# A hybrid decoder step: the token mixer of the next tile divided into pieces and placed between the expert groups of the present tile

## The chip, the cores and the metric

The kernel runs on one core of a Trainium2 chip. The metric is the device time of one execution in microseconds (us). The core's engines work side by side and meet through semaphores: TensorE (PE; its weight loads are listed as PEld), VectorE (DVE), ScalarE (ACT), GpSimd (POOL) and SyncE (SP). Sixteen DMA engines move data between HBM and the on-chip memory.

## The reference, cut to what matters

One decoder layer is computed for 1024 prompt tokens and for 8 sample tokens (one new token of each of 8 sequences with a cache). All data are float32, the width is 1024.

```
h   = rmsnorm(x) * (1 + sc1) + sh1                 # six modulation vectors from silu(c) @ w_ada + b_ada
rq, rk, rv, rg, aq, ak, av = split(h @ w_in)       # 7 x 512 columns, 8 heads of 64 each
ret = groupnorm(retention(rq, rk, rv)) * silu(rg)  # chunks of 128 tokens, state carried from chunk to chunk
att = dilated_window_attention(norm(aq), norm(ak), av)   # softmax with counts and distances, over all earlier tokens
x   = x + gt1 * (concat(ret, att) @ w_out)
h2  = rmsnorm(x) * (1 + sc2) + sh2
for each of 8 heads of each token:                 # product-key experts
    s1, s2 = the two halves of (h2 @ w_pq) times sub_keys;  16 best sums s1[i] + s2[j] -> 16 experts, gates g
    y += sum over the 16 experts of  g * gelu(u_e . h2) * v_e
x   = x + gt2 * y
```

Outputs are the new rows of the prompt and of the samples, the retention states, and the keys and values. The attention of a tile needs the keys of all earlier tiles, and the retention needs the state left by the tile before. The experts of a token need only its own h2.

## The kernel before, in words

The tokens are worked on in 8 tiles of 128 (`T = 8`). Three functions follow one another, each a block that ends with all engines meeting.

`front` first computes the modulation: twelve chunks of w_ada of 2 MiB stream through three buffers (L207, L527). It then runs the mixer in a loop over the 8 tiles. For each tile, nine chunks of 2 MiB (7 of w_in, 2 of w_out, 512 columns each) stream through the same three buffers; the products are L577 (w_in) and L662 (w_out). TensorE makes the score products (L608) of a head, VectorE adds the distances and takes the maximum (`att_max`, L420), ScalarE takes the exponential (L314), TensorE turns the probabilities (L633), VectorE multiplies them by the counts (`att_weigh`, L431), and TensorE makes the weighted sum of the values (L647). Two pairs of PSUM banks hold the scores of two heads. The number of keys is rounded up to a multiple of 256. At the end of a tile the residual `x_mid` and the normed row `h2` are stored to HBM (L251, L252).

`decode` does the mixer of the 8 sample rows, with its own pass over w_in and w_out and a gathered part of the cache.

`peer` does the experts. Queries, turned queries and scores of a head are made by TensorE four heads ahead (L1259, L1265, L1270), and VectorE chooses the 16 experts two heads ahead, in eight parts (`choose_next`, L1368 to L1412). A row of `uv` holds an expert's u and v, 8 KB. GpSimd gathers one expert for each of the 128 tokens into one of eight ring buffers (`gather`, L1145), 1 MiB at a time, 16 times a head. The ring is used in groups of two slots:

```
for q in range(GROUPS):                     # 8 groups of a head; 8 heads, 8 tiles: 512 groups
    DVE : wait gathered;  dot[s] = sum(ring[s][u] * h2)      # L1448, twice
    ACT : act_h = gelu(dot)                                  # L1230
    DVE : act_h = act_h * gate / sum(gates)                  # L1457
    DVE : one of the eight parts of the choice for head n + 2
    ACT : ring[s][v] = ring[s][v] * act_h[s]                 # L1190, twice
    PE  : psum += turned ring[s][v], 8 blocks                # L1325; then the two slots are free
    POOL: wait free;  gather two more
```

Every engine runs its part of this in its own written order. At the end of a tile VectorE waits for the sum (L1337), scales it, TensorE turns it back (L1342), and VectorE adds it to `x_mid` (L1464, L1468); SP stores y (L1136) and loads the next h2 (L1132). The loops over tiles and heads are loops of the engines.

## Time and profile before

| | us |
|---|---|
| median of 3 runs | 3856.61 |
| lowest and highest | 3854.44, 3859.69 |
| the profiled execution | 3865.25 |
| its span, first to last instruction | 3863.6 |
| TensorE, VectorE, ScalarE, GpSimd busy | 2684.1, 2437.5, 1676.4, 1270.9 |
| mean granted TensorE clock (1 is 2.4 GHz) | 0.827 |

Busy time counts the instructions of an engine that compute; the idle time before an instruction is put down to whoever released it. The DMA share is the mean busy share of the sixteen DMA engines. A span is from the first to the last instruction, so the profiled execution's own time is a little longer.

### The profile page before, as it was taken

What the parts mean: (1) busy time and instruction counts of PE and PEld (TensorE: products, weight loads), DVE (VectorE), ACT (ScalarE), POOL (GpSimd) and SP (SyncE); (2) the same over time, 40 slices, a digit from 0 to 9 for tenths busy, and PEclk for the clock granted to TensorE, in tenths of its full rate; (3) what the DMA queues carried; (4) which work ended last, traced back from release to release, by engine and by line L of the source; (5) the groups of instructions that cost most, each with busy time, mean ns of one, the idle gap of its engine ahead of it and who ended that gap; (6) DMA issues with size and microseconds to landing.
All of it is one profiled execution on the core that took longest, in us unless ns stands there. A gap on an engine that the chain in (4) does not pass through costs nothing.

```text
span 3863.6 us, 42539 instructions
## 1 busy us (share of the span) xinstructions
PE 2684.1 (69%) x13275; PEld 1978.7 (51%) x13275; DVE 2437.5 (63%) x5982; ACT 1676.4 (43%) x2367; POOL 1270.9 (33%) x1089
## 2 busy tenths in 40 slices
PE   8999999999666656666656666665666566566656
PEld 2445545555124555555555555555555555555554
DVE  0333234444137777777777777777777777777776
ACT  0221122222104555555455555555555555555553
POOL 0000000000003544444444444444544444444443
PEclk9888899999878878777778787778878777787778
DMA  8566665543748999999999999999999999999998
GB/s 305 207 223 223 223 221 201 193 155 128 263 170 328 421 401 398 422 401 421 393 420 407 407 422 404 422 396 402 422 398 422 401 422 406 406 422 400 422 405 346
DMA packets 264246, 1337.37 MB, mean 346 GB/s; under 512 B 23681, under 2 KB 24033, under 8 KB 130833
## 3 DMA queue, kind: packets, MB, share of 16 engines
q0 software_dynamic: 152832, 1096.88, 68.8%
q1 hardware_dynamic: 111376, 240.00, 17.1%
q8 instruction: 23, 0.38, 0.0%
q14 instruction: 15, 0.12, 0.0%
HBM read 1318.03 MB, written 18.77 MB: 346 GB/s over the span
## 4 chain that ended last, share of the span: by engine, by line
DMA 32%; issue 14%; PE 12%; ACT 6%; DVE 5%; POOL 1%; ACTq 0%; POOLq 0%; DVEq 0%; SPq 0%
DMA pr_ring<-uv,pr_expert 31%; PE pair L1325 10%; ACT pr_ring L1190 4%; DVE pr_ring L1448 2%; POOL pr_ring L1145 1%; ACT pr_act_h L1230 1%; DVE pr_act_h L1457 1%; PE pair L1337 0%; PE pair L1349 0%; PE pair L1292 0%; PE bank L1259 0%; DMA pr_wpq<-w_pq 0%; DVE pr_dot L1448 0%; ACT L1230 0%; ACT L1225 0%
## 5 line engine op out<-in xcount | busy, mean ns | idle before, releaser
L1325 PE MATMUL pair<-sb_ident,pr_ring 128*128 128x128 f32 x8192 | 1383.4, 340 | 1030.3 <-ACT pr_ring L1190 1030.2
L1325 PEld LDWEIGHTS pair<-sb_ident,pr_ring 128*128 128x128 f32 x8192 | 1237.2, 178 | 1178.3 <-ACT pr_ring L1190 1178.3
L1145 POOL DMA_INDIRECT pr_ring<-uv,pr_expert x1024 | 1223.6, 1195 | 1470.7 <-PE pair L1325 1232.9
L1448 DVE CUSTOM_DVE_ANT_0 pr_ring<-pr_ring,pr_h2cur 128x1024 f32<-128x1024 f32 x1024 | 1250.4, 1226 | 319.9 <-DMA pr_ring<-uv,pr_expert 270.0
L1190 ACT ACTIVATE pr_ring<-pr_ring,pr_act_h 128x1024 f32<-128x1024 f32 x1024 | 1120.0, 1141 | 147.9 <-DVE pr_act_h L1457 147.9
L1230 ACT ACTIVATE pr_act_h<-pr_dot 128x2 f32<-128x2 f32 x512 | 104.1, 203 | 1004.1 <-DVE pr_dot L1448 1001.8
L577 PE MATMUL pair<-sb_w,sb_hT 128*128 128x512 f32 x896 | 388.6, 592 | 1.4 <-ACT sb_b2row L288 1.4
L577 PEld LDWEIGHTS pair<-sb_w,sb_hT 128*128 128x128 f32 x896 | 168.9, 190 | 208.4 <-issue 208.4
L1457 DVE SCALAR_TENSOR_TENSOR pr_act_h<-pr_act_h,pr_gsum,pr_gate_h 128x2 f32<-128x2 f32 x512 | 113.1, 221 | 174.1 <-ACT pr_act_h L1230 174.1
L1259 PE MATMUL bank<-pr_wpq,pr_h2T 128*128 (+1 forms) x1088 | 167.7, 320 | 9.8 <-DMA pr_wpq<-w_pq 9.8
L1259 PEld LDWEIGHTS bank<-pr_wpq,pr_h2T 128*128 128x128 f32 x1088 | 166.4, 241 | 10.8 <-DMA pr_wpq<-w_pq 10.2
L251 POOL DMA_DIRECT2D x_mid<-sb_qk x8 | 4.9, 611 | 498.2 <-DVE sb_sp L504 498.2
L314 ACT ACTIVATE sb_sp<-sb_sp,sb_st 128x256 f32<-128x256 f32 (+3 forms) x64 | 53.1, 829 | 162.3 <-DVE sb_st L423 162.2
L662 PE MATMUL pair<-sb_w,sb_turned 128*128 128x512 f32 x256 | 119.4, 627 | 5.7 <-ACT sb_turned L324 5.7
L647 PEld LDWEIGHTS bank<-sb_va,sb_pt 128*128 128x128 f32 x640 | 87.4, 214 | 60.9 <-DVE sb_pt L431 50.2
L647 PE MATMUL bank<-sb_va,sb_pt 128*128 128x65 f32 x640 | 97.2, 305 | 22.5 <-DVE sb_pt L431 22.3
L245 POOL DMA_DIRECT2D wk_prompt<-sb_qkn x8 | 4.6, 570 | 307.6 <-DVE sb_qkn L399 307.6
L608 PE MATMUL pair<-sb_kT,sb_turned 64*128 64x512 f32 (+1 forms) x192 | 95.0, 604 | 0.0
L527 PE MATMUL bank<-sb_w,sb_cT 128*9 128x512 f32 x192 | 86.5, 605 | 10.0 <-DMA sb_w<-w_ada 10.0
L495 DVE TENSOR_TENSOR sb_qk<-pair,sb_gt1row 128x512 f32<-128x512 f32 x16 | 11.1, 692 | 126.7 <-PE pair L662 126.7
L662 PEld LDWEIGHTS pair<-sb_w,sb_turned 128*128 128x128 f32 x256 | 50.9, 202 | 70.2 <-issue 62.0
L1448 DVE DVE_READ_ACCUMULATOR2_ANT pr_dot<- 128x1 f32 x1024 | 84.1, 82 | 0.0
(300 smaller groups left out, 2314.6 us busy)
## 6 DMA issues: line engine op xcount, KB each, us to landing
sb_w<-w_in SPq DMA_DIRECT2D x56, 2048.0 KB, 8.2
sb_w<-w_out SPq DMA_DIRECT2D x16, 2048.0 KB, 7.7
sb_w<-w_ada SPq DMA_DIRECT2D x12, 2048.0 KB, 7.9
pr_ring<-uv,pr_expert POOLq DMA_INDIRECT x1024, 10.1
de_w<-w_in SPq DMA_DIRECT2D x7, 2048.0 KB, 12.8
sb_xt<-x_all SPq DMA_DIRECT2D x9, 512.0 KB, 11.1
pr_h2next<-h SPq DMA_DIRECT2D x9, 512.0 KB, 8.3
sb_mix<-x_all SPq DMA_DIRECT2D x8, 512.0 KB, 3.4
```

The lines of the kernel that those rows point to most:

```text
L527: last = pe.matmul(ps[c % 2][0:NC9, :], cT[:, k, :], w[c % WBUF][:, k, :], start=(k == 0), stop=(k == KT - 1))
L577: last = pe.matmul(bank, hT[:, k, :], w[c % WBUF][:, k, :], start=(k == 0), stop=(k == KT - 1))
L608: last = pe.matmul(psS[h % 2][:, c], aqT[e, h // 2, :], kT[e, h // 2, c], start=True, stop=True)
L647: last = pe.matmul(psO[h // 4][:, (h % 4) * VA:(h % 4) * VA + VA], pt[h % 2][:, k * P:(k + 1) * P], va[:, k, h * VA:(h + 1) * VA], start=( ...
L662: last = pe.matmul(psS[0][:, n * 512:(n + 1) * 512], mixT[:, k, :], w[c % WBUF][:, k, :], start=(k == 0), stop=(k == KT - 1))
L1145: pool.indirect_dma_start(ring[r][:], None, a["uv"], bass.IndirectOffsetOnAxis(ap=index, axis=0)).then_inc(s_g[r], 16)
L1190: last = act.activation(ring[s % RING][:, D:2 * D], ring[s % RING][:, D:2 * D], ACT.Identity, scale=act_h[:, s:s + 1])
L1230: act.activation(act_h[:, c], dot[:, c], ACT.Gelu).then_inc(s_gelu, 1)
L1259: last = pe.matmul(ps[0][:, 0:P], h2T[:, k, :], wpq[:, k, ds(h * P, P)], start=(k == 0), stop=(k == KT - 1))
L1325: last = pe.matmul(psS[0][:, k * P:(k + 1) * P], ring[s % RING][:, D + k * P:D + (k + 1) * P], ident[:], start=False, stop=False, is_trans ...
L1448: last = dve.tensor_tensor_reduce(ring[r][:, 0:D], ring[r][:, 0:D], h2cur[:], 1.0, 0.0, ALU.mult, ALU.add, dot[:, s:s + 1])
L1457: dve.scalar_tensor_tensor(out=act_h[:, c], in0=act_h[:, c], scalar=gsum[u][:, 1:2], in1=gate_h[u][:, c], op0=ALU.mult, op1=ALU.mult)\
```

## The change

The three functions become `condition`, `decode` and `layer`. `condition` is the modulation part of the former `front`. `decode` also makes the queries and scores of the sample rows (two more chunks, of w_pq), and stores three modulation rows to HBM. `layer` is one block for mixer and experts. Its loops are written out. Each engine has a generator `front()` that yields the group number at which its next piece of a mixer is due, and a `Pace` that runs the pieces that are due after each group of its expert loop. Tile 0's mixer is due before everything, tile 1's runs two pieces a group from group 0, and tile t's begins 32 groups before tile t - 1's experts begin:

```diff
+    def when(t, o):
+
+        return -1 if t == 0 else o // 2 if t == 1 else (t - 1) * STEPS - STEPS // 2 + o
+    class Pace:
+        def __init__(self, pieces):
+            self.pieces = pieces
+            self.due = next(pieces, None)
+        def upto(self, g):
+            while self.due is not None and self.due <= g:
+                self.due = next(self.pieces, None)
...
+            for n in range(N):
+                t, h = n // HP, n % HP
+                for q in range(GROUPS):
...
+                    pe.wait_ge(s_dg, n * GROUPS + q + 1)
+                    for s in range(q * GRP, q * GRP + GRP):
+                        for k in range(KT):
+                            last = pe.matmul(psA[:, k * P:(k + 1) * P],
+                                             ring[s % RING][:, D + k * P:D + (k + 1) * P], ident[:],
...
+                    last.then_inc(s_free, 1)
+                    if q == 6 and n + AHEAD < N:
+                        peer_scores(n + AHEAD)
+                    pace.upto(n * GROUPS + q)
```

The pieces of a mixer have numbers o from 0 to 68: on TensorE the turned x (5), 14 projection chunks (6 to 19), retention (21, 23), four pairs of heads in seven steps each (from 23), the last head (52), the turned mix (54), four w_out chunks (55 to 58), the turned h2 (62), four w_pq chunks (63 to 66), the turned queries (68). VectorE's and ScalarE's pieces lie at the same numbers or one or two behind:

```diff
+                    for c in range(NIN):
+                        yield when(t, 6 + c)
...
+                        product(t, c, hT)
+                        if c == 7:
+                            pe.wait_ge(s_qkn, t + 1)
+                            turn(qk, 0, KT).then_inc(s_T, 1)
...
+                    for pair in range(4):
+                        p = 23 + 7 * pair
+                        yield when(t, p)
+                        scores(2 * pair)
+                        if pair >= 1:
+                            yield when(t, p + 1)
+                            weighted(2 * pair - 1)
+                        yield when(t, p + 2)
+                        scores(2 * pair + 1)
+                        yield when(t, p + 5)
+                        turn_probs(2 * pair)
+                        yield when(t, p + 6)
+                        weighted(2 * pair)
+                        turn_probs(2 * pair + 1)
```

and on VectorE `att_max` at p + 1 and p + 3 and `att_weigh` at p + 6 and p + 8; on ScalarE both exponentials of a pair at p + 4.

The weights of every tile, w_pq among them, stream in chunks of 256 columns (`CW`) instead of 512 (1 MiB, in rows of 1 KB) through three buffers (`NB`), 22 chunks a tile, on SP's queue, in one written order with the other loads and stores of a tile:

```diff
+    w = [sb(f"w{i}", [P, KT, CW]) for i in range(NB)]
...
+            for t in range(T):
+                first = t * NCH + NB
+                for c in range(first, first + 8):
+                    chunk(c)
+                store_keys(t)
+                for c in range(first + 8, t * NCH + NIN):
+                    chunk(c)
+                store_values(t)
+                if t >= 2:
+                    store_y(t - 2)
+                if t >= 1:
+                    load_mid(t - 1)
+                for c in range(t * NCH + NIN, t * NCH + NIN + NB):
+                    chunk(c)
+                load_rows(t)
+                if t + 1 < T:
+                    load_x(t + 1)
+                for c in range(t * NCH + NIN + NB, t * NCH + NCH):
+                    chunk(c)
+                store_mid(t)
+                if t + 1 < T:
+                    for c in range((t + 1) * NCH, (t + 1) * NCH + NB):
+                        chunk(c)
```

`chunk(i)` waits until product i - 3 is done. `load_rows` loads the three modulation rows as broadcasts (they had stayed on chip) and x a second time, after waits for the gated retention output and for the last head's product. PSUM holds the expert sum (one pair of banks), one pair for scores and projections, one for turned blocks, and two single banks. The keys are exactly (t + 1) x 128. h2 stays on chip in two buffers; x_mid still goes through HBM. At the end of an expert tile VectorE waits for the freed ring, scales the sum, and adds it, after the first dot products of the next tile. The choice for the sample rows runs during head 62, and their h2 rows are spread near the end.

## Rows read from the trace of the kernel before

**Rows 1.** The page: busy time, share of the span, instructions.
```profile
PE 2684.1 (69%) x13275; PEld 1978.7 (51%) x13275; DVE 2437.5 (63%) x5982; ACT 1676.4 (43%) x2367; POOL 1270.9 (33%) x1089
```

**Rows 2.** Stages: start:end, us, busy of each engine, clock, DMA share, GB/s.
```profile
0.00:104.20 104.20, 91.10 (x248) 21.52 (x248) 3.99 (x13) 10.67 (x18) 7.83 (x8) 1.00 0.81 294
104.20:975.00 870.80, 818.75 (x2956) 451.15 (x2956) 345.77 (x691) 187.30 (x298) 18.07 (x32) 0.94 0.54 196
975.00:1126.40 151.40, 104.43 (x291) 31.95 (x291) 37.92 (x55) 14.09 (x23) 11.51 (x16) 0.84 0.59 207
1126.40:1190.00 63.60, 41.59 (x152) 22.24 (x152) 31.43 (x120) 10.01 (x25) 7.64 (x8) 0.74 0.75 291
...
1521.40:3508.60 1987.20, 1213.02 (x7202) 1089.35 (x7200) 1504.41 (x3812) 1090.87 (x1500) 920.06 (x768) 0.78 0.99 410
...
3828.00:3863.60 35.60, 22.91 (x60) 7.90 (x60) 15.81 (x32) 4.00 (x11) 3.72 (x4) 0.82 0.52 215
```

**Rows 3.** The page: the chain that ended last, by engine.
```profile
DMA 32%; issue 14%; PE 12%; ACT 6%; DVE 5%; POOL 1%; ACTq 0%; POOLq 0%; DVEq 0%; SPq 0%
```

**Rows 4.** 300 us inside an expert tile: window, dot products, GpSimd's wait.
```profile
2200.00:2500.00 300.00, 181.14 (x1089) 164.46 (x1087) 230.72 (x587) 167.11 (x231) 147.72 (x121) 0.79 1.00 415
```
```profile
L1448 DVE CUSTOM_DVE_ANT_0 pr_ring<-pr_ring,pr_h2cur 128x1024 f32<-128x1024 f32 x118 | 144.2, 1225 | 38.1 <-DMA pr_ring<-uv,pr_expert 32.7 <-DVE pr_pos L1370 1.5 <-DVE pr_pos L1374 1.4
```
```profile
POOL pr_ring L1145 <- PE pair L1325: 130.5, 51, 9.2
```

**Rows 5.** Stores of y, first to last; waits at tile ends, 1400 to 3600.
```profile
L1136 SPq DMA_DIRECT2D y_prompt<-pr_xmid x8: 355/356/364, 1521.5 to 3839.8; - x8
```
```profile
DVE pr_yT L1464 <- PE pair L1337: 48.2, 7, 8.3
```

**Rows 6.** Timeline (start, us): sample stage begins; a head's choice; sample queries.
```profile
984.05 0.36 SPq L766 DMA_DIRECT2D de_xs<-x_sample  x1
...
1148.29 0.30 DVE L1368 MAX8 pr_top<-pr_sc 128x8 f32<-128x128 f32 x1 [21.07 <-ACT pr_sc L1184]
...
1153.83 15.60 PE L1292 MATMUL pair<-pr_wpq,pr_h2sT 128*8 128x512 f32 x32 [0.31 <-ACT pr_h2sT L1204]
...
1159.14 0.17 DVE L1412 CAST pr_expert<-pr_expert_f 128x16 uint32<-128x16 f32 x1
```

**Rows 7.** Products of w_in and w_out: ns min/median/max, first and last start.
```profile
L577 PE MATMUL pair<-sb_w,sb_hT x896: 592/592/692, 114.6 to 901.3; 128*128 128x512 f32 x180
```
```profile
L662 PE MATMUL pair<-sb_w,sb_turned x256: 592/592/1222, 198.7 to 965.6; 128*128 128x512 f32 x128
```

**Rows 8.** The mixer, groups by line and shape: busy us, mean ns | idle before.
```profile
L577 PE MATMUL pair<-sb_w,sb_hT 128*128 128x512 f32 x896 | 388.6, 592 | 1.4 <-ACT sb_b2row L288 1.4
...
L431 DVE TENSOR_TENSOR sb_pt<-bank,sb_count_t 128x512 f32<-128x512 f32 x64 | 42.7, 688 | 26.7 <-PE bank L633 25.7 <-DVE sb_osb L439 0.4
...
L420 DVE CUSTOM_DVE_ANT_0 sb_sp<-pair,sb_dist_t 128x768 f32<-128x768 f32 x16 | 15.3, 957 | 8.8 <-PE pair L608 8.6
L314 ACT ACTIVATE sb_sp<-sb_sp,sb_st 128x768 f32<-128x768 f32 x16 | 15.0, 936 | 40.3 <-DVE sb_st L423 40.2
...
L420 DVE CUSTOM_DVE_ANT_0 sb_sp<-pair,sb_dist_t 128x512 f32<-128x512 f32 x16 | 11.0, 690 | 10.2 <-PE pair L608 10.1
```
```profile
L314 ACT ACT_TABLE_LOAD x16 | 20.5, 1283 | 0.3
```

**Rows 9.** The page: DMA queue, kind: packets, MB, share of 16 engines.
```profile
q0 software_dynamic: 152832, 1096.88, 68.8%
q1 hardware_dynamic: 111376, 240.00, 17.1%
```

**Rows 10.** Timeline of an expert group: two GELUs and a dot product that waited.
```profile
2215.43 0.20 ACT L1230 ACTIVATE pr_act_h<-pr_dot 128x2 f32<-128x2 f32 x1 [2.29 <-DVE pr_dot L1448]
...
2219.14 1.22 DVE L1448 CUSTOM_DVE_ANT_0 pr_ring<-pr_ring,pr_h2cur 128x1024 f32<-128x1024 f32 x1 [0.73 <-DMA pr_ring<-uv,pr_expert]
...
2220.41 0.20 ACT L1230 ACTIVATE pr_act_h<-pr_dot 128x2 f32<-128x2 f32 x1 [2.03 <-DVE pr_dot L1448]
```

More of the change, by code:

```diff
@@ L29 @@
 CHUNKS = NPROJ + 2
-SEG = 2
 WBUF = 3
@@ L177, in front @@
[L177 to L188 removed]
+        s_chain = sem("ada_step")
@@ L667, in decode, with _, step @@
-def decode(nc, a, sem, ps, psS, psO, ident, tabs):
+        @block.vector
+        def _(dve):
+            steps = [0]
+            def step(ins):
+                steps[0] += 1
+                ins.then_inc(s_chain, 1)
+                dve.wait_ge(s_chain, steps[0])
+            dve.wait_ge(s_adaT, ADA_CHUNKS)
+            dve.wait_ge(s_const, 48)
+            step(dve.tensor_tensor(mod[:], psO[1][:, 0:48 * NC9].rearrange("p (m c) -> p m c", c=NC9),
+                                   badaT[:].unsqueeze(2).to_broadcast([P, 48, NC9]), ALU.add))
+            sec = [mod[:, s * KT:(s + 1) * KT, :] for s in range(6)]
+            for n, (sc, sh, gt) in enumerate(((1, 0, 2), (4, 3, 5))):
+                gb = gnT[:, n, :].unsqueeze(2).to_broadcast([P, KT, NC9])
+                step(dve.scalar_tensor_tensor(out=tabs[:, 3 * n, :, :], in0=sec[sc], scalar=1.0, in1=gb,
+                                              op0=ALU.add, op1=ALU.mult))
+                step(dve.tensor_copy(tabs[:, 3 * n + 1, :, :], sec[sh]))
+                dve.tensor_copy(tabs[:, 3 * n + 2, :, :], sec[gt]).then_inc(s_tabs, 1)
+            dve.wait_ge(s_tabs, 2)
@@ L766, in _ @@
             sp.dma_start(xs[:], a["x_sample"]).then_inc(s_xs, 16)
-            for c in range(CHUNKS):
+            for c in range(LOADS):
                 if c == WBUF:
@@ L1345, in _, with product @@
[L1345 to L1349 removed]
+            def product(t, c, lhs):
+                i = t * NCH + c
+                pe.wait_ge(s_w[i % NB], 16 * (i // NB + 1))
+                at = (c % 4 if c < NIN else (c - NIN) % 4) * CW
+                for k in range(KT):
+                    last = pe.matmul(psS[:, at:at + CW], lhs[:, k, :], w[i % NB][:, k, :],
+                                     start=(k == 0), stop=(k == KT - 1))
+                last.then_inc(s_pj, 1)
```

1507 lines of the change are left out of this document (698 added, 809 removed).

## The prediction

> **What bounds the kernel now.** I read the stage table first [rows 2]: conditioning 104 us, the mixer over its eight tiles 871, the sample rows 151, the expert stage's setup 64, the eight expert tiles 2638 (1190.0 to 3828), the end 36 [rows 2]. In the mixer TensorE is busy 94% of the stage and the DMA engines 54%; among the experts TensorE is at 61% and the DMA engines at 99%. Two stages with opposite limits, one after the other, and no engine above 69% of the whole span [rows 1]. The chain agrees: its largest share is DMA [rows 3].
>
> Inside an expert tile: in 300 us VectorE did 118 dot products, 2.53 us each, so 5.05 us for a group of two [rows 4]. The same stretch moved 415 GB/s at a DMA share of 1.00. VectorE waited for a gather 32.7 us, 0.55 a group, so it could run a group in 4.50: its slack is only 0.55. GpSimd waits for TensorE to free a slot, which is what a full ring looks like. A tile lasts 331.2 us (y stores, [rows 5]); 64 groups of 5.05 are 323, and 8 are lost at the tile's end, where VectorE waits for TensorE.
>
> **The change, part by part.** I follow the time line of the new kernel.
>
> 1. Conditioning: the same twelve weight chunks, 104 plus 2 for the block's end: 106.
>
> 2. Sample rows: 142 us lie between the stage's first load (984.05) and its end (1126.4) [rows 2, 6]. The sample queries move here from the expert setup. Their 32 instructions take 15.6 us [rows 6], and with transposes, copies and scores in series I take 22: ends at 106 + 142 + 22 = 270.
>
> 3. Tile 0's mixer runs alone, then two heads' choices. Load, norm, turn and scale of x: 15. From first projection to first output product the present tile 0 takes 198.7 - 114.6 = 84 [rows 7]; the new one has 128 keys instead of 256 and one score buffer instead of two, so I keep 84, and add 5 for the turn of the mix. A chunk of 256 columns is 16 instructions of half of 434 ns (388.6 us by 896, [rows 8]), 3.5 us; four for w_out 14, four for w_pq 14. Residual, norm and h2: 8. Turns and copies around them: 9. The choice of one head is 11 us (1148.29 to 1159.31, [rows 6]), two of them 22. Sum 171, plus 11 for TensorE starts at the lower clock: 182. First dot product at 452, against 1190 now: 738 us earlier.
>
> 4. The 512 groups keep their 2638 us, and seven tiles of mixer come on top. First the DMA work. A tile streams 22 chunks of 1 MiB in 1 KB pieces (present pieces: 2 KB). The queues' rows give two packet prices [rows 9]: 61,818 engine-us times 68.8% by 152,832 is 278 ns for 7,177 B, and times 17.1% by 111,376 is 95 ns for 2,155 B. A line through them is 16 ns plus 0.0365 ns a byte: 54 ns for 1,024 B, 3.43 us a chunk over 16 engines, 75 a tile. No row shows a 1 KB stream; bounds are bytes at the gather's 415 GB/s (2.53) and the 2 KB packet's price for the smaller packet (6.07). I take the line, since both ends of it fit. x twice, three broadcast rows, stores of x_mid, keys and values, less the h2 load, are 3.1 MB: 8, and 2.5 for short pieces. Together 86 a tile, 602 in seven. Nothing hides it, since the DMA engines are full.
>
> 5. What VectorE adds. In projection and output steps each chunk makes the DMA pay 3.4 us, and VectorE's additions there (about 20 us a tile) lie under it. The steps from the mask to the mix (22 to 54 of 69, 33 groups) have no such cover. At 640 keys, the mean of tiles 1 to 7, a head's maximum is 0.82 us (0.69 at 512 keys, 0.96 at 768) plus 0.3 for readout and sign, its weighting 0.85 (0.69 for 512 columns) [rows 8]: 4.1 a pair of heads. The exponentials of a pair cost ScalarE 2 x 0.83 (0.94 at 768 keys) plus two table loads of 1.28: 4.2. It sits idle 2.03 to 2.29 before a GELU, of which 0.73 is VectorE's own wait for a gather [rows 10]: some 1.4 are free once that wait is gone. So GELU, and VectorE behind it, is 2.8 late a pair. TensorE's probabilities and scores come a step before they are read: 1.5 of waits a pair. Four pairs: 34. Retention output, centering, deviation and gate 7.7, mask 1.3, row sums 1.4, ScalarE's mix scaling 1.5, retention's product late 4, and the end of the peer tile, now in this stretch, 6.6: 56 in all. VectorE needs 33 x 4.50 + 56 = 205. DMA needs 33 x 5.05 = 167, plus three prefetched chunks 10 and small transfers 7: 184. VectorE ends last by 21; the 8 of the present tile end go: net 13 a tile, 91. Tile 1's pieces run two a group, so waits a step apart fall into one step: 10 more. Sum 101.
>
> 6. TensorE is busy 202 us in an expert tile (1213.02 by 6) and 102 in a mixer tile (818.75 by 8), of which 49 are projections [rows 2, 8]. A new tile holds at most 202 + 76 of products + 38 of the mixer's rest = 316 of some 430, 73%: no bound. The granted clock was 0.78 among the experts and 0.94 in the mixer, so denser work should raise it.
>
> 7. SP and GpSimd. Chunks, stores, x and row loads now share SP's queue in one written order. Behind y's store (waiting for the previous tile's sum) stand the w_out chunks, released at step 32, needed at 55; the fourth w_out chunk stands behind the wait for the last head's product, and is asked for three steps before use. TensorE will wait there, and the ring's transposes behind it, but chunks then fill the DMA engines: it costs nothing beyond their 75. GpSimd loses its stores.
>
> 8. Sample rows spread and chosen during the last tiles, once 10 us of DMA (4.2 MB) and 6 of VectorE: 16. End: 36 as now.
>
> Sum: 452 + 2638 + 602 + 101 + 16 + 36 = 3845. The profiled execution took 3865.25 for a span of 3863.6, and the median is 8.6 below it: 3845 + 1.65 - 8.6 = **3838 us**. The trade is 738 earlier for some 719 back.
>
> The Trainium skill's "DMA: Bandwidth & Descriptors", section Specifications, puts line rate at 512 B and above and the fabric at 435 GB/s. By it a chunk is an estimated 2.4 us, and the sum falls by about 157 to some 3681. The trace already differs from that rule [rows 9]: 2 KB packets ran at 363 GB/s, 7 KB ones at 413. The same skill's "ScalarE: Activation LUTs", section What ACT_TABLE_LOAD costs, adds a 1.38 us drain to each switch; with the eight switches of a tile's pairs that would be an estimated 11 a tile, 77 in all, and the sum some 3915: on A's side, and I leave it in A's chance. No row I read shows a drain of its own.
>
> **Rivals.**
> A, slower: lockstep. Each tile has eleven waits of VectorE and ScalarE for a projection chunk (pieces 8, 10, 12, 14, 16, 18, 20, 57, 59, 65, 67). I count them hidden under DMA. If one product, 3.5 us, is exposed at each because the ring's four groups can't bridge it, a tile gains 39, seven 270: 4108. It decides from 19 / 7 = 2.7 us a tile. For it: slack 0.55 a group, in-order queues, one score buffer. Against: a chunk step takes the DMA 8.5 us and VectorE 4.5.
> B, cheap weights: two queues hide the packet's fixed time, and a chunk costs its bytes. 154 x 0.90 = 139 less: 3699. For it: share 1.00 with one busy queue says nothing of two.
> C, dear weights: 1 KB packets cost what 2 KB ones do, 154 x 2.64 = 407 more: 4245. Also where slow weights starve TensorE with the DMA idle.
> That the overlap doesn't happen at all would leave the stages' sum, 3857 or more; pieces are written between the groups, so I give this nothing.
>
> **How the numbers follow.** Forecast (0.58): 3770 to 3910 by the uncertainty of the 21 and of tile 0, faster in 0.36, same 0.07, slower 0.15. B 0.14, faster. A 0.18, whole or in part, and C 0.10: slower. So faster 0.50, same 0.07, slower 0.43; 0.2% (7.7 us) is about what a measurement of this kernel can tell from no change. The range goes from B, 3690, to 4020, which takes in A's smaller half and leaves out C and A whole, under 0.2.
>
> **What the profile will show.** The first dot product near 452; steady tiles of about 430 us against 331; DMA share 0.95 or more outside steps 22 to 54 and about 0.9 within; hardware-queue packets near 54 ns at 1 KB; VectorE's waits for gathers gone in attention steps and replaced by waits for ScalarE; last 92 groups at 5.05. The prediction is wrong if the packet's price is, if tile 0 alone takes over 220, or if DMA idles in the chunk steps.

## The result and the profile after

The changed kernel takes 3925.7 us, the median of four runs from 3911.7 to 3942.3, against 3857.4 (3854.4 to 3859.7) before, taken on the same chip. The ratio is 1.0179, with a 95% interval of 1.0139 to 1.022: 1.8% slower, where 3838 and a small gain were forecast. The time lies within the forecast's range (3690 to 4020); the direction does not agree. The profiled execution is the fastest of the four, 3911.7 us for a span of 3909.9. The forecast's sum for a profiled execution was 3845, so 65 us have to be found.

The page of the changed kernel: busy time of each engine, two rows of its queues (packets, MB, share of 16 engines' time), and the chain that ended last, by engine and by line. They answer to [rows 1, 3, 9].

```profile
PE 2641.9 (68%) x13651; PEld 2177.5 (56%) x13651; DVE 2331.0 (60%) x5816; ACT 1770.7 (45%) x2366; POOL 1122.8 (29%) x1054
...
q0 software_dynamic: 149072, 1083.68, 69.6%
q1 hardware_dynamic: 234512, 287.23, 21.6%
...
PE 32%; DMA 20%; DVE 19%; ACT 18%; issue 3%; POOL 1%; DVEq 0%; POOLq 0%
PE pairA L1134 15%; PE pairS L986 12%; ACT pr_ring L968 10%; DMA pr_ring<-uv,pr_expert 10%; DVE pr_ring L1395 9%; DMA pr_w<-w_in 4%; DMA pr_w<-w_out 3%; DMA pr_w<-w_pq 3%; PE pairT L992 2%; ACT L965 2%; DVE pr_act_h L1411 1%; PE pairS L1053 1%; ACT pr_act_h L965 1%; POOL pr_ring L855 1%; ACT pr_sp L922 1%
```

No compute engine is near full over the span, and the DMA engines are at 91% (69.6 + 21.6), against 86% before [rows 9]. The chain, whose largest share before was DMA [rows 3], now goes round: TensorE's transposes (L1134) and products (L986), ScalarE's scaling (L968), the gather, VectorE's dot products (L1395).

The stages come from a table of stretches, the form of [rows 2]. They are conditioning, sample rows, tile 0's mixer, and then stretches from one y store to the next: the first, second, fourth, seventh and eighth expert tile.

```profile
core 0: us, PE busy (x) PEld busy (x) DVE busy (x) ACT busy (x) POOL busy (x), PEclk, DMA share, GB/s
0.00:102.70 102.70, 89.94 (x240) 20.66 (x240) 1.78 (x7) 8.59 (x15) 0.21 (x5) 1.00 0.72 257
102.70:265.00 162.30, 126.28 (x355) 38.92 (x355) 37.90 (x54) 17.20 (x28) 9.71 (x15) 0.86 0.60 211
265.00:432.10 167.10, 115.05 (x496) 94.32 (x496) 52.45 (x158) 26.22 (x53) 11.84 (x11) 0.77 0.65 211
432.10:961.80 529.70, 356.55 (x1880) 312.62 (x1880) 299.52 (x760) 241.80 (x326) 132.32 (x128) 0.79 0.89 332
961.80:1392.40 430.60, 290.80 (x1590) 256.89 (x1590) 280.55 (x712) 218.78 (x291) 139.29 (x128) 0.79 0.97 378
1833.10:2266.70 433.60, 299.70 (x1654) 265.43 (x1654) 284.43 (x713) 220.58 (x291) 134.73 (x128) 0.79 0.97 374
3164.70:3544.20 379.50, 243.76 (x1364) 214.79 (x1364) 267.54 (x670) 199.97 (x259) 142.60 (x128) 0.77 0.96 382
3544.20:3881.80 337.60, 186.18 (x1040) 165.50 (x1040) 238.42 (x593) 172.11 (x224) 146.58 (x127) 0.76 0.99 405
```

The overlap exists. The first dot product starts at 432.1 against some 1190 before. But an expert tile that carries a whole tile of mixer takes 430.7, 440.7, 433.5, 444.3 and 453.7 us, 440.6 on average, against 331 alone. The first, which carries one and a half, takes 530. In these six the DMA share is 0.89 to 0.97, not the 1.00 of an expert tile before [rows 4], and they move 332 to 378 GB/s where the last tile, without a mixer, moves 405. No engine fills the rest: TensorE and VectorE are at 57 to 70%.

Where in a tile is the time lost? The same view, cut at the starts of dot products (L1395) that belong to given steps of a mixer: steps 22 to 31, steps 32 to 54, and then the steps with products, 55 to 68 and on to step 21 of the next mixer.

```profile
2194.20:2260.70 66.50, 47.03 (x257) 40.67 (x258) 50.32 (x122) 36.05 (x45) 22.01 (x22) 0.72 0.86 330
2260.70:2391.00 130.30, 87.43 (x514) 76.62 (x511) 101.75 (x256) 75.43 (x95) 48.37 (x45) 0.79 1.01 408
2391.00:2634.40 243.40, 165.67 (x904) 147.53 (x904) 133.29 (x335) 109.65 (x154) 67.33 (x63) 0.84 0.95 359
```

The forecast had the exposed waits in steps 22 to 54, and there the DMA engines are full from step 32 on. The 31 groups with products, in which it took them to be full, have a share of 0.95 and take 243.4 us.

The waits of the changed kernel (engine, line, releaser: us in total, times, longest) show who stands still:

```profile
DVE pr_act_h L1411 <- ACT pr_act_h L965: 603.5, 505, 17.0
...
DVE pr_qk L1320 <- PE pairS L986: 133.1, 16, 16.0
ACT pr_sp L939 <- PE pairS L986: 119.9, 16, 18.3
DVE pr_ring L1395 <- DMA pr_ring<-uv,pr_expert: 118.1, 127, 2.7
DVE pr_qk L1192 <- PE pairS L986: 106.6, 16, 10.1
...
PE pairS L986 <- DMA pr_w<-w_in: 51.8, 15, 7.9
...
PE pairS L986 <- DMA pr_w<-w_out: 47.4, 6, 12.6
...
PE pairS L986 <- DMA pr_w<-w_pq: 44.9, 6, 13.1
```

Before, VectorE waited 174 us for the GELU and 270 for gathers. Now it waits 604 for the GELU (L965) and 118 for gathers: the data is there, and ScalarE isn't. To this come 240 us in which VectorE waits for a product (L1192, L1320), 120 in which ScalarE does (L939), and 144 in which TensorE waits for a chunk.

One such wait, from the timeline of the changed kernel (start, duration, and in brackets the idle time and its releaser), projection step 8 of a tile:

```profile
2090.22 1.91 PE L1134 MATMUL pairA<-sb_ident,pr_ring 128*128 128x128 f32 x16
...
2090.85 2.19 ACT L968 ACTIVATE pr_ring<-pr_ring,pr_act_h 128x1024 f32<-128x1024 f32 x2 [0.37 <-DVE pr_act_h L1411]
...
2091.97 3.62 PE L986 MATMUL pairS<-pr_w,pr_hT 128*128 128x256 f32 x16
...
2095.42 1.91 PE L1134 MATMUL pairA<-sb_ident,pr_ring 128*128 128x128 f32 x16
2095.69 0.69 DVE L1192 COPY pr_qk<-pairS 128x512 f32<-128x512 f32 x1 [4.88 <-PE pairS L986]
2096.30 1.22 DVE L1395 CUSTOM_DVE_ANT_0 pr_ring<-pr_ring,pr_h 128x1024 f32<-128x1024 f32 x1
...
2098.70 0.20 ACT L965 ACTIVATE pr_act_h<-pr_dot 128x2 f32<-128x2 f32 x1 [5.66 <-DVE pr_dot L1395]
```

TensorE does the transposes of its group at 2090.22 and then the product, 2091.97 to 2095.6. VectorE's copy of that product is due one group later, and VectorE is there at once: it had come to L1192 at 2090.82 and stands 4.88 us, until 2095.69. Its next dot product starts at 2096.30, so ScalarE's next GELU stands 5.66 us (2098.70), and TensorE's next transposes, GpSimd's slots and the gathers behind them are late in turn. TensorE works on a group after VectorE and ScalarE have finished with it. A piece written "one step later" on VectorE is therefore not one step later in time.

### The profile page after: what moved, and what is told of

Same layout as the page of the kernel before. It is cut to its first block, busy times and chain, and to the rows that moved or that the text cites. A ratio compares the mean times of both kernels' runs of the same rounds, so it can differ in the third digit from the quotient of the medians.

```text
span 3909.9 us, 37947 instructions
## 1 busy us (share of the span) xinstructions
PE 2641.9 (68%) x13651; PEld 2177.5 (56%) x13651; DVE 2331.0 (60%) x5816; ACT 1770.7 (45%) x2366; POOL 1122.8 (29%) x1054
## 3 DMA queue, kind: packets, MB, share of 16 engines
q0 software_dynamic: 149072, 1083.68, 69.6%
q1 hardware_dynamic: 234512, 287.23, 21.6%
## 4 chain that ended last, share of the span: by engine, by line
PE 32%; DMA 20%; DVE 19%; ACT 18%; issue 3%; POOL 1%; DVEq 0%; POOLq 0%
PE pairA L1134 15%; PE pairS L986 12%; ACT pr_ring L968 10%; DMA pr_ring<-uv,pr_expert 10%; DVE pr_ring L1395 9%; DMA pr_w<-w_in 4%; DMA pr_w<-w_out 3%; DMA pr_w<-w_pq 3%; PE pairT L992 2%; ACT L965 2%; DVE pr_act_h L1411 1%; PE pairS L1053 1%; ACT pr_act_h L965 1%; POOL pr_ring L855 1%; ACT pr_sp L922 1%
## 5 line engine op out<-in xcount | busy, mean ns | idle before, releaser
L1134 PE MATMUL pairA<-sb_ident,pr_ring 128*128 128x128 f32 x8192 | 1389.6, 341 | 1009.7 <-ACT pr_ring L968 1006.4
L1134 PEld LDWEIGHTS pairA<-sb_ident,pr_ring 128*128 128x128 f32 x8192 | 1251.8, 180 | 1156.4 <-ACT pr_ring L968 1125.2
L855 POOL DMA_INDIRECT pr_ring<-uv,pr_expert x1024 | 1099.7, 1074 | 2492.2 <-PE pairA L1134 2175.9
L1395 DVE CUSTOM_DVE_ANT_0 pr_ring<-pr_ring,pr_h 128x1024 f32<-128x1024 f32 x1024 | 1222.6, 1222 | 135.3 <-DMA pr_ring<-uv,pr_expert 118.1
L968 ACT ACTIVATE pr_ring<-pr_ring,pr_act_h 128x1024 f32<-128x1024 f32 x1024 | 1120.1, 1141 | 157.3 <-DVE pr_act_h L1411 157.3
L986 PE MATMUL pairS<-pr_w,pr_hT 128*128 128x256 f32 x2304 | 572.3, 407 | 101.9 <-DMA pr_w<-w_in 51.8
L965 ACT ACTIVATE pr_act_h<-pr_dot 128x2 f32<-128x2 f32 x512 | 104.6, 204 | 1111.1 <-DVE pr_dot L1395 1109.2
L986 PEld LDWEIGHTS pairS<-pr_w,pr_hT 128*128 128x128 f32 x2304 | 468.9, 208 | 177.3 <-DMA pr_w<-w_pq 46.3
L986 PE MATMUL pairS<-pr_w,pr_turned 128*128 128x256 f32 x512 | 135.4, 426 | 51.9 <-DMA pr_w<-w_out 47.4
L986 PEld LDWEIGHTS pairS<-pr_w,pr_turned 128*128 128x128 f32 x512 | 109.5, 219 | 71.3 <-DMA pr_w<-w_out 48.8
L1053 PE MATMUL pairS<-pr_kTva,pr_turned 64*128 64x512 f32 (+3 forms) x192 | 95.9, 614 | 6.8 <-DVE pr_st L1224 6.8
L146 PE MATMUL pairT<-ad_w,ad_cT 128*9 128x512 f32 x192 | 86.5, 605 | 9.9 <-DMA ad_w<-w_ada 9.9
L1320 DVE TENSOR_TENSOR pr_qk<-pairS,pr_rows 128x512 f32<-128x512 f32 x16 | 11.1, 692 | 133.1 <-PE pairS L986 133.1
L1395 DVE DVE_READ_ACCUMULATOR2_ANT pr_dot<- 128x1 f32 x1024 | 84.3, 82 | 0.0
L1192 DVE COPY pr_qk<-pairS 128x512 f32<-128x512 f32 x16 | 11.1, 692 | 106.6 <-PE pairS L986 106.6
## 6 DMA issues: line engine op xcount, KB each, us to landing
pr_w<-w_in SPq DMA_DIRECT2D x112, 1024.0 KB, 14.8
pr_w<-w_out SPq DMA_DIRECT2D x32, 1024.0 KB, 26.3
```

Of the source, the lines that this page charges most:

```text
L146: last = pe.matmul(ps[c % 2][0:NC9, :], cT[:, k, :], w[c % WBUF][:, k, :], start=(k == 0), stop=(k == KT - 1))
L855: pool.indirect_dma_start(ring[r][:], None, a["uv"], bass.IndirectOffsetOnAxis(ap=index, axis=0)).then_inc(s_g[r], 16)
L965: act.activation(act_h[:, c], dot[:, c], ACT.Gelu).then_inc(s_gelu, 1)
L968: last = act.activation(ring[s % RING][:, D:2 * D], ring[s % RING][:, D:2 * D], ACT.Identity, scale=act_h[:, s:s + 1])
L986: last = pe.matmul(psS[:, at:at + CW], lhs[:, k, :], w[i % NB][:, k, :], start=(k == 0), stop=(k == KT - 1))
L1053: last = pe.matmul(psS[:, c], aqT[e, h // 2, :], kT[e, h // 2, c], start=True, stop=True)
```

## The experiments

In the table the tile is the mean of the second to sixth expert tile, each with one mixer tile, read from the y stores of each run's trace. "First" is the first expert tile, from the first dot product to the first y store; it carries one and a half mixers.

| kernel | median us | against before | tile us | first us |
|---|---|---|---|---|
| before | 3857 to 3863 | | 331 | |
| changed | 3925.7 | 1.018 | 440.6 | 530 |
| 1 packed weights | 3764.5 | 0.974 | 417.5 | 512 |
| 2 before, packed | 3861.5 | 1.001 | | |
| 3 weights once | 3697.7 | 0.958 | 406.0 | 508 |
| 4 no other tables | 3852.5 | 0.997 | 430.0 | |
| 5 packed, head start 1 | 3620.2 | 0.937 | 404.5 | |
| 6 packed, head start 2 | 3796.7 | 0.982 | 432.2 | |
| 7 packed, slot handover | 3617.2 | 0.936 | 397.2 | |
| 8 weights once, no other tables | 3616.7 | 0.937 | 392.4 | |
| 9 packed, head start 1 and slots | 3586.8 | 0.930 | 398.7 | 434 |
| 10 head start 1 | 3734.0 | 0.968 | 418.5 | 472 |
| 11 head start 1 and slots | 3729.6 | 0.967 | 420.8 | |
| 12 before, slot handover | 3808.7 | 0.987 | 324.1 | |
| 13 head start, products only | 3786.0 | 0.980 | 427.1 | |
| 14 head start, attention only | 3882.1 | 1.006 | 437.7 | |
| 15 slot handover | 3780.5 | 0.978 | 423.6 | |
| 16 packed, products 2, attention 1 | 3662.8 | 0.949 | 410.4 | |

**1. Packed weights.** The host stores each chunk as 128 rows of 8 KB; bytes, order and waits stay.

```diff
-                if c < NIN:
-                    at = ORDER[c // 2] * HW + (c % 2) * CW
-                    src = w_in[:, :, at:at + CW]
...
+                src = a["w_packed"][c]
...
+    r["w_packed"] = cols.reshape(KT, P, -1, 256).transpose(2, 1, 0, 3)
```

> Only the layout of the streamed weights in memory changes: each chunk is stored as 128 rows of 8 KB, so that its packets are as large as a gather's. Theory D (the DMA engines are full and the weights pay for their small packets): a chunk costs its bytes, 2.5 us, in place of 57.6 ns x 64 = 3.7 us; 154 chunks give back some 180 us, 3745. The share of the DMA engines in the steps of the output product stays at 0.88. Theory L (latency: the queues alternate packet by packet, so a chunk of 1024 small packets waits behind 1024 large ones and lands in 15 to 26 us, TensorE waits for it, the scale-and-add chain behind TensorE stops and the DMA engines run dry): chunks land in 5 to 8 us, TensorE's 284 us of waits for w_in, w_out and w_pq fall below 60, the share of the output steps rises to 0.97 or more, and that adds some 100 to 140 us to the 180: 3605 to 3645. Theory S (ScalarE's table loads and the late GELU set the pace): less than 60 us of gain, above 3865.

It gained 161 us, 1.05 a chunk for 154 chunks, and is faster than the kernel before the change. That is near theory D's 180. The rows of DMA issues (KB each, median us from issue to landing) of the changed kernel, and of this one:

```profile
pr_w<-w_in SPq DMA_DIRECT2D x112, 1024.0 KB, 14.8
pr_w<-w_out SPq DMA_DIRECT2D x32, 1024.0 KB, 26.3
pr_w<-w_pq SPq DMA_DIRECT2D x32, 1024.0 KB, 18.8
```

```profile
pr_w<-w_packed SPq DMA_DIRECT2D x176, 1024.0 KB, 9.6
```

The same bytes land in 9.6 us in place of 14.8 to 26.3, and TensorE's waits for chunks fall from 144 to 2 us (the expectation's 284 counts the waits of the weight loads, 140, a second time). Theory L had the direction of this right, but its 100 to 140 us on top did not come: the tile still takes 417.5. So TensorE's waits for chunks were mostly not what held the end.

**2. The control.** The kernel before, its mixer reading packed chunks (`src = a["w_packed"][c]`). Its chunks are of 2 MiB, so that the rows grow from 2 to 16 KB.

> The control: the kernel before the change, with w_in and w_out of its mixer stage in the packed layout (w_pq there is loaded once and stays as it is). Its mixer is bound by TensorE at 94% with the DMA engines at 54%, and in its expert stage no weights move. All theories: no change, 3857 within 10 us. If it gains more than 20, packed weights help for a reason that has nothing to do with the overlap.

Ratio 1.0006 (0.9995 to 1.0016). In a stage whose DMA share is 0.54 the packing is worth nothing.

**3. Weights once.**

```diff
+                if t >= 1:
+                    spq.dma_start(w[i % NB][:, 0, 0:4], src[:, 0, 0:4]).then_inc(s_w[i % NB], 16)
+                else:
+                    spq.dma_start(w[i % NB][:], src).then_inc(s_w[i % NB], 16)
```

> After tile 0 each chunk load is replaced by one of 16 bytes a partition into the same buffer, with the same waits and signals; later tiles so multiply with stale weights. What is left out is 154 MiB of weight traffic. It is the floor for the schedule with free weights. Theories D and L: 64 groups of 4.5 us plus VectorE's additions of a tile (20 in product steps, 56 in steps 22 to 54) make some 365 a tile in place of 435, so seven tiles gain 490: some 3440; no waits for weights. Theory S: steps 22 to 32 keep their 6.4 us a group and the whole gains under 300 us, above 3620.

Theories D and L missed, and this run changed my mind. With the weights almost free the kernel takes 3697.7, not 3440. Theory S said above 3620 and, as before, 6.4 us a group in steps 22 to 32. Both came about: the ten groups of steps 22 to 31 take 66.5 us (mean of the second to sixth tile), and 67.0 in the changed kernel. Whether the table loads are the reason is the next question. This run's first, fourth and last expert tile:

```profile
432.60:940.40 507.80, 350.24 (x1880) 309.27 (x1880) 299.57 (x760) 241.73 (x326) 134.67 (x128) 0.79 0.75 280
1741.40:2147.60 406.20, 292.20 (x1654) 260.19 (x1654) 283.50 (x712) 220.56 (x291) 136.14 (x128) 0.81 0.89 342
3331.60:3670.40 338.80, 186.41 (x1040) 164.18 (x1040) 237.61 (x592) 172.00 (x223) 141.35 (x129) 0.75 0.99 404
```

The DMA share is 0.75 and 0.89 in tiles that carry mixer. A tile is still 75 us longer than one without, and the first one is 508. DMA isn't what bounds it there; some coupling of the engines is. (The stale weights also change which experts are chosen; the last tile, without a mixer, takes 338.8 where it took 337.5, so the gathers cost what they did.)

**4 and 8. No other tables.** In the pieces, `ACT.Identity` for `ACT.Sqrt`, `ACT.Silu` and the attention's `ACT.Exp` (there with `scale=0.0`), once on the changed kernel and once on run 3's.

> In the mixer's pieces every function of ScalarE that needs another table than GELU's (Sqrt, Silu, the attention's Exp) is replaced by Identity, with as many instructions over as many elements; the mixer's values are then wrong. 67 table loads there and 63 for the GELU after them go, 167 us of ScalarE in all. Theory S: nearly all of it was on the path of VectorE's 604 us of waits for the GELU, 120 to 170 us of gain, some 3775. Theories D and L: only the part in steps 22 to 54 of the tile, where DMA is not full, four pairs with 2 loads each of which 1.4 are hidden: at most 8 us a tile, 20 to 60 us in all, 3865 to 3905.

> Weights loaded in full only for tile 0 (what the 3698 us run left out) and, in the mixer's pieces, Identity in place of Sqrt, Silu and Exp. With the DMA engines relieved, the price of the 130 table loads (167 us) should show in full if ScalarE holds VectorE up. Theory S: 110 to 160 us below 3698, some 3560. Theory K: part of the loads lies in waits for TensorE anyway: 40 to 90 below, some 3635. Theory D: under 30 below.

They gained 73 us (run 4's times spread from 3812 to 3873) and 81 us (3611 to 3623), about half of the 167 us that left ScalarE. That is less than theory S said both times, more than D and L said for run 4, and within theory K's 40 to 90 for run 8. The table loads are a real part, of like size with and without weight traffic, but with them gone a tile of run 8 still takes 392.

**5 and 6. Head start.** TensorE's mixer pieces are due one group earlier (run 5) or two (run 6, `o - 2`); nothing else moves. In tile 1's mixer, with two pieces a group, it is half of that. On packed weights.

```diff
         def _(pe):
+            def due(t, o):
+                return when(t, o - 1)
...
-                        yield when(t, 6 + c)
+                        yield due(t, 6 + c)
```

> Packed weights, and every mixer piece of TensorE is due one group earlier than before, those of the other engines stay. TensorE handles a group one to two steps after VectorE did (dot, GELU, coefficient, scaling, transposes), so a piece of VectorE or ScalarE due one step behind TensorE's piece waits for it, while TensorE's waits for theirs have slack. Theory K (lockstep: distances of one step between engines that run two steps apart): VectorE's and ScalarE's waits for products, turns and scores (some 440 us in the packed kernel) halve, and 10 to 25 us a tile come back: 3600 to 3690. Theory R (the ring of four groups is a loop whose latency, transfer and all engines' pieces included, sets the pace): the waits move to other names, gain under 20, above 3745. Theory D (DMA-bound): no change within 15 of 3765.

> The same with two groups earlier. Theory K: another 0 to 40 us below the run with one group, since the natural lag of TensorE is one and a half to two steps; then TensorE's own waits for VectorE and ScalarE start to show and it may turn. Theories R and D: no change within 20 of 3765.

One group gave 144 us more (3764.5 to 3620.2), as theory K said. VectorE's wait for the GELU fell from 489 to 290 us, its wait for gathers rose from 213 to 487: the transfers are last again, as they should be in a stage that DMA bounds. The head start also makes the chunks be asked for earlier, since a chunk waits for a product to be done; but TensorE's waits for packed chunks were 2 us before and 4 after, so this is not where the 144 us come from. The second group lost 176 us, more than the first had gained. The waits of that run:

```profile
PE bank L1065 <- DVE pr_pt L1229: 190.6, 43, 9.2
...
ACT pr_sc L943 <- PE bank L1112: 127.5, 38, 5.9
```

With one group these were 94.2 and 11.2. TensorE now comes to the attention's products before VectorE has weighted the probabilities, stands in front of its own transposes, and holds up the experts' scores of a later head behind them. The best of the three distances is one group. All theories missed the second one: K had 0 to 40 us of further gain, R and D no change.

**7. Slot handover.** ScalarE, TensorE and GpSimd pass the ring on in single slots.

```diff
-                    last.then_inc(s_dg, 1)
+                                       scale=act_h[:, s:s + 1]).then_inc(s_dg, 1)
...
-                    pe.wait_ge(s_dg, n * GROUPS + q + 1)
                     for s in range(q * GRP, q * GRP + GRP):
+                        pe.wait_ge(s_dg, n * TOPK + s + 1)
...
-                    last.then_inc(s_free, 1)
+                        last.then_inc(s_free, 1)
...
-                    if s % GRP == 0 and j >= RING // GRP:
-                        pool.wait_ge(s_free, j - RING // GRP + 1)
+                    if j >= RING:
+                        pool.wait_ge(s_free, j - RING + 1)
```

> Packed weights, and ScalarE, TensorE and GpSimd hand over single slots of the ring in place of groups of two: TensorE begins after the first scaling (1.1 us earlier), GpSimd starts a gather when the first slot is read (2.2 to 2.7 us earlier). No instruction is added or taken. Theory R: a slot's loop of about 4 x 5.5 us is shortened by 3 in 22, so stretches with mixer pieces run up to 10% faster: 100 to 200 us less, 3560 to 3670. Theory K: the groups are held by engine waits, not by the ring: under 40 us of gain, above 3725. Theory D: none.

147 us (3764.5 to 3617.2), theory R's size. Together with run 9, where the two edits don't add up, this says that the ring's length and the pieces' distance are two handles on the same loop.

**9. Both, on packed weights.**

> Packed weights with both edits: TensorE's mixer pieces one group earlier, and the ring handed over slot by slot. Each alone gave some 145 us on the packed kernel (3620 and 3617). Theory K+R (two parts of one loop: the pieces' waits and the ring's own length; once it is short enough the DMA engines are the bound): no sum of the two but a stop near the DMA's price, 432 + 2638 + 7 x (22 x 2.6 + 8) + 36, about 3560, so 3540 to 3590 with DMA share 0.97 or more in every stretch. If the two are independent: 3475. If they are one and the same: 3610.

3586.8 us, 0.930 of before (0.928 to 0.932), the fastest of all and within theory K+R's range: 30 and 33 us below either edit alone, where independent parts would have given 3475. Its first, fourth and last expert tile:

```profile
428.90:863.40 434.50, 332.99 (x1883) 292.40 (x1883) 300.64 (x761) 241.28 (x326) 139.72 (x128) 0.85 0.99 404
1653.30:2051.10 397.80, 291.07 (x1654) 256.96 (x1654) 286.06 (x712) 220.35 (x292) 148.83 (x128) 0.83 1.00 409
3213.70:3551.50 337.80, 197.04 (x1040) 171.16 (x1040) 237.80 (x592) 172.18 (x224) 146.96 (x128) 0.73 0.99 403
```

The DMA share is 0.98 to 1.01 in every tile. A tile of 398.7 is 331 plus 68, and 22 chunks of 2.53 us with the 10.5 for small transfers are 66. Even the first tile, one and a half mixers, takes 434 where the changed kernel took 530. Here DMA is the bound to within 2 or 3%, and the lockstep is gone but for what these hide.

**10, 11 and 15. The same edits on the change as it was made**, with 1 KB pieces: head start, head start and slots, slots alone.

> The change as it was made, weights in pieces of 1 KB, with TensorE's mixer pieces one group earlier as the only edit. Theory K (the lockstep of neighbouring pieces is what the change lost): 3926 falls by 100 to 170 us, to about 3790, which is faster than before the change. Theory L (with small packets TensorE waits for the chunks themselves, so an earlier piece only waits longer): it falls by under 40, above 3885.

> The change as it was made, weights in 1 KB pieces, with both edits. Theory K+R: it ends at what DMA takes, about 432 + 2638 + 7 x 86 + 36 = 3708 by the forecast's own price of a chunk, 3680 to 3740. Theory L: chunks that land in 15 to 26 us keep it above 3780.

> The change as made, with only the slot-by-slot handover. On packed weights it gave 147 us. Theory R (a longer ring absorbs any engine's late piece): 120 to 170 us, some 3780. If the small packets' late chunks cap it: 60 to 120, some 3840. With both edits on 1 KB pieces 3730 was the end, so it can't go below.

3734.0, 3729.6 and 3780.5. The head start alone turns 1.8% slower into 3.2% faster, and gains more than theory K's 100 to 170 us. Its first, fourth and last expert tile, then steps 22 to 54 and the steps with products of the tile shown above, and its waits:

```profile
432.90:905.30 472.40, 330.05 (x1882) 289.36 (x1882) 300.25 (x760) 241.24 (x326) 138.04 (x128) 0.84 0.97 371
1736.90:2153.90 417.00, 288.22 (x1654) 254.66 (x1654) 284.65 (x712) 220.51 (x291) 139.60 (x128) 0.81 1.00 390
3365.60:3702.80 337.20, 186.99 (x1040) 165.97 (x1040) 237.61 (x592) 172.00 (x223) 145.87 (x127) 0.77 0.99 405
...
2087.20:2281.60 194.40, 134.01 (x764) 117.76 (x762) 153.16 (x378) 111.61 (x139) 71.38 (x68) 0.76 0.97 387
2281.60:2507.20 225.60, 161.10 (x896) 142.99 (x896) 133.98 (x334) 109.54 (x154) 66.46 (x60) 0.83 1.00 384
```

```profile
DVE pr_act_h L1414 <- ACT pr_act_h L965: 430.7, 506, 14.2
DVE pr_ring L1398 <- DMA pr_ring<-uv,pr_expert: 284.3, 272, 4.2
PE pairS L989 <- DMA pr_w<-w_in: 181.8, 32, 14.7
...
DVE pr_qk L1195 <- PE pairS L989: 102.1, 11, 15.7
...
PE pairS L989 <- DMA pr_w<-w_out: 78.5, 7, 13.6
```

The share is 1.00 in the fourth tile, and a tile takes 418.5, that is 331 + 87. The steps with products take 225.6 us at a share of 1.00, where the changed kernel took 243.4 at 0.95. What is instructive: TensorE's waits for chunks rise from 144 to 311 us (181.8 + 78.5 + 50.9) while the kernel gets 192 us faster. TensorE comes earlier, waits longer, and the product is still done sooner: VectorE waits 192 us for products (102.1 at L1195 and 89.9 at L1323) where it waited 240. Theory L took the waits for chunks for the cause. Slots on top give only 4 us more, less than the spread of the runs (3722 to 3744), with the share at 0.96 to 0.99. Slots alone (run 15) give 145 us, theory R's size again.

**12. Slots on the kernel before.**

> The control: the kernel before the change with slot-by-slot handover in its expert stage. There DMA share is 0.99 and the ring is long enough. All theories: 3860 within 15. If it gains over 40, the ring's length held the kernel before too and the comparison of the packed kernels has to be read anew.

I was wrong here: 3808.7, 50 us less (0.987, 0.985 to 0.990). One of its expert tiles:

```profile
1835.30:2159.30 324.00, 204.10 (x1201) 179.07 (x1200) 251.38 (x636) 181.89 (x250) 135.09 (x128) 0.79 1.01 419
```

324.0 us are 64 groups of 5.06, so the 8 us at each tile's end, which I had named and taken as given, are gone. Eight times 7 is the 50 and a little more; the packed kernels' gain of 147 is three times that, so the reading of run 7 stands for the larger part. The share is worth a look too: 1.01 here, 0.99 before. Those two hundredths are the 7 us.

**13 and 14. Which pieces.** The head start only where it moves products and turns, and only in retention and attention.

```diff
+            def due(t, o):
+                return when(t, o - (0 if 21 <= o <= 52 else 1))
```

This is run 13; in run 14 the 0 and the 1 are exchanged.

> The change as made; of TensorE's pieces only the turns and products of steps 5 to 20 and 54 to 68 are one group earlier, those of retention and attention stay. Theory A (the eleven waits for products are the loss): nearly all of the 192 us, 3735 to 3790. Theory B (the attention's pairs, which the DMA doesn't cover, are the loss, as forecast step 5 had it): under 70, 3860 to 3926.

> The other half: only the pieces of steps 21 to 52 are one group earlier. Theory A: under 70 us, 3860 to 3926. Theory B: most of the 192, 3735 to 3790. If both halves give their share, the two runs' gains add up to about 190.

140 and 44 us; together 184 of the 192, as theory A and the sum had it. Three quarters come from the products' steps.

The same by stretches, from the starts of the dot products in each trace (mean of the second to sixth tile; the forecast's row is its own sum, 429 less 205):

| kernel | 31 groups with products | 33 groups, steps 22 to 54 |
|---|---|---|
| forecast | 224 | 205 |
| changed | 242.4 | 198.2 |
| 10 head start 1 | 225.6 | 192.5 |
| 13 products only | 228.1 | 199.0 |
| 14 attention only | 247.2 | 190.1 |
| 3 weights once | 211.3 | 194.9 |
| 9 packed, head start and slots | 207.5 | 190.8 |

Each half of the head start shortens its own stretch and not the other.

**16. Two groups for products, one for attention**, on packed weights.

> Packed weights, products and turns two groups earlier, retention and attention one. If the loss of the run with two groups everywhere (3797 against 3620 with one) is in the attention's chain, where TensorE's piece then waits for VectorE's weighting, this run stays at 3600 to 3640; if it is in the products' steps, it is above 3700.

3662.8, between the two expectations: 43 us above run 5, and 134 below run 6. Three quarters of what the second group costs is in the attention's chain, so the expectation's first case holds in the main, though its 3600 to 3640 were too low.

## Why the prediction was wrong, step by step

- **Steps 1 to 3** held within 5, 5 and 15 us: conditioning ends at 102.7 (106 forecast), the sample rows at 265.0 (270), tile 0 and two choices take 167 (182; 11 of these were for a low clock, and no row gave that figure). The first dot product came 20 us sooner than forecast. That error was to the good.
- **Step 4**, the DMA's price, was right. In run 10 the 31 groups with products take 225.6, at a share of 1.00 in the tile shown; by the forecast 31 groups of 5.05 and the mixer's 86 less the 17 of the other steps are 226. Over the whole tile 418.5 and 420.8 (runs 10 and 11) against 331 are 87 and 90. That is a little kind to it: the 331 hold the tile's end, which run 12 does without, and against its 324 they are 94 and 97. Part of the difference lies in steps 22 to 54, where run 10's share is 0.97. Hardware-queue packets took 57.6 ns on average (21.6% of 16 x 3909.9 us by 234,512), at 1,225 B a packet on average, for which the line gives 61; no view gives the 1,024 B packets by themselves. Pieces of 8 KB save 0.93 us a chunk between runs 11 and 9 (143 us by 154), both nearly full, and the forecast's two ends, 3.43 and 2.53, differ by 0.90. (A reading was slightly off: 118 dot products in 300 us are 2.54 each and 5.08 a group, not 5.05; run 12's tile gives 5.06.)
- **Step 5 failed.** It compared two sums, VectorE's 205 us and DMA's 184, in steps 22 to 54, took the difference, and put everything in the product steps under DMA, at a price of nothing. Net 13 a tile. That is right only if the longer of two workers always has something to do. Here they are tied by a ring of four groups and by in-order queues. The stretches show it: the product steps, 224 by the forecast, took 242.4, 18 more, and 225.6 with the head start; steps 22 to 54, 205 by the forecast, took 198.2, 7 less. So the one stretch in which the forecast saw an exposed engine was shorter than it said, and the other, in which it saw none, held the loss. The whole tile says the same: with almost free weights the schedule needs 406 (run 3), with the DMA nearly full 418; it took 440.6, more than either, since each engine stands still at times when another is late: share 0.94 to 0.97, and 0.89 in the first tile.
- **The 65 us in the terms of the sum.** A tile alone is 2638 / 8 = 330 and a full one 330 + 86 + 13 = 429. The five full tiles took 12 more each, 59. The first was to take 330 + 1.5 x 99 + 10 = 488 and took 520 to its last dot product (530 to the store, 10 behind it): 32. With the 20 gained at the first dot product, 8 gained in the last tile and 2 lost at the end, that makes the 65. The net of 12 a tile is smaller than the mistake by luck, since 7 us too many elsewhere stood against the 18. The table loads come near in size, and part of that is luck as well: the forecast's 2.8 us late per pair of heads are 11 a tile and 78 in seven, and the removal gave 73 and 81; but the runs removed 18 or 19 loads a tile, of which the forecast had counted 8.
- **The argument against rival A was the same error.** It said that a chunk step gives DMA 8.5 us of work and VectorE 4.5, so a product's 3.5 would be hidden. But a wait of VectorE is not paid out of DMA's budget: no slot comes free while it stands, and after four groups no gather is left to run. A's "decides from 2.7 us a tile" was passed many times over: one group of head start gives back 22 us in a steady tile (440.6 to 418.5), 17 of it in the product steps, and 57 in the first. A's 39 a tile was too much, its mechanism was the one that decided the sign. I gave it 0.18, on the ground of the very budget argument that step 5 used.
- **Rivals B and C** were bounds of a price that the line had right. The part of C in which slow weights starve TensorE exists (144 us of waits), but what it took is not isolated. Packing is worth 161 us on the change as made, 163 with slots (3780.5 to 3617.2), 143 with head start and slots, and 114 with head start alone (3734.0 to 3620.2). If the 143 are the price of the packets alone, late chunks took some 20 us of the 161 and 163; but the 114 show that this price isn't paid in full everywhere, so the 20 are an estimate and no bound.
- **Step 6**: TensorE at 67 to 70% in the tiles with mixer was no bound, as forecast. That its clock would rise was wrong: the windows show 0.79 with mixer pieces and 0.76 in the last tile, against 0.78 among the experts before. Run 10 shows 0.84 and 0.81, run 9 0.85 and 0.83; whether that came from the denser work was not tested.
- **Step 7**: the fourth w_out chunk was indeed waited for (w_out chunks land in 26.3 us in the median). It said that this costs nothing beyond the chunk's own price. SP's order was not varied, so whether that is so stays open.
- **Steps 8 and end**: the last dot product at 3872.0, the end 38 us later (36 forecast). The last expert tile took 337.5 where 346 was forecast. Its first eight groups took 53.6 us and the others 39.6 to 40.8 by eights, 5.0 to 5.1 a group: 13 us lie where the sample rows are spread, not 16, and the 8 of the tile's end, which the sum had struck out only in the tiles with a mixer, are gone here too.
- **What the profile would show**: the steady tiles were to take about 430 (440.6), DMA share 0.95 or more outside steps 22 to 54 and 0.9 within. In the tile shown it is 0.95 outside, and within it 0.86 up to step 31 and 1.01 from there on. VectorE's waits for gathers gone and replaced by waits for ScalarE: right, and it should have warned me, because it is the signature of a loop that is not bound by DMA any more.

The rule in the Trainium skill's "DMA: Bandwidth & Descriptors", section Specifications, that pieces of 512 B and more run at line rate does not hold in these runs. By it packing could change nothing; 8 KB pieces instead of 1 KB pieces were worth 143 and 161 us. The drain of 1.38 us that the Trainium skill's "ScalarE: Activation LUTs", section What ACT_TABLE_LOAD costs, adds to each load is not to be seen either. The load in the changed kernel's timeline starts 0.02 us after the activation before it, and the next activation starts right at its end:

```profile
2086.97 0.38 ACT L949 ACTIVATE pr_sc<-bank 128x256 f32<-128x256 f32 x1
2087.37 1.28 ACT L958 ACT_TABLE_LOAD   x1
...
2088.66 0.21 ACT L958 ACTIVATE pr_gate_h<-pr_delta 128x16 f32<-128x16 f32 x1
```

## What to carry to other kernels

When a second job is threaded through a ring that DMA keeps full, add up each engine's work, but don't subtract one sum from another: count, for each hand-over between engines, how many groups late the sending engine's own place in the loop is, and give it that head start and no more. Here TensorE handles a group behind VectorE, so its pieces had to be due one group earlier; that one change was worth 192 us, and a second group cost 176 on packed weights. Then free ring slots one by one as they are read (145 and 147 us without the head start, 4 and 33 with it), and lay streamed weights out in pieces as long as those of the transfers they share the engines with.

## What the hardware showed that was not expected

- Beside gathers of large packets a 1 MiB chunk in 1 KB pieces lands in 14.8 to 26.3 us (medians, queueing behind other chunks included), in 8 KB pieces in 9.6, though the bytes are the same. A 2 MiB chunk in the mixer of the kernel before, with no gathers beside it, lands in 8.2 (w_in) and 7.7 (w_out).
- Alone in its stage, at a share of 0.54, longer pieces change nothing (ratio 1.0006).
- The share of the DMA engines can be 0.94 to 0.97 over a tile in which they still lose 20 us: 1.01 is what full looks like here (run 12, 419 GB/s), 0.99 hid 7 us in 331 (the kernel before), and 0.96 is a sign of a wait, not of a bound.
